# Even projection: each odd tile is turned one product later, and the mixer's first inputs are loaded by the projection

## The reference

```
def ssd_diffattn_mixer(u, w_in, w_out, conv_w, conv_b, ...):
    z, xBC, dt, q, k, v, g = jnp.split(u @ w_in, idx, axis=-1)
    xBC = jax.nn.silu(causal_dwconv(xBC, conv_w, conv_b))
    xs, Bm, Cm = jnp.split(xBC, [SSD_WIDTH, SSD_WIDTH + SSD_GROUPS * SSD_STATE], axis=-1)
    ...
    y = ssd_scan(xs, dt, A, Bm, Cm) + xs * D_skip[:, None]
    y_a = rmsnorm(y * jax.nn.silu(z), ssd_norm_w)
    ...
```

## Time and profile before

| | us |
|---|---|
| median of 3 runs | 4179.75 |
| lowest and highest | 4172.42, 4181.28 |
| the profiled execution | 4173.78 |
| its span | 4172.1 |
| PE busy in it | 3789.3 (91%) |
| DVE, ACT, POOL busy | 2280.9, 1805.1, 1562.0 |
| granted TensorE clock, mean | 0.952 of full |

### The profile page before, as it was taken

How to read it: one execution, slowest core, us unless ns; L and a number is a source line. 1 busy time by engine, 2 the same in 40 slices (tenths; PEclk the granted TensorE clock), 3 DMA queues, 4 the chain that set the end, 5 groups by cost and what they waited for, 6 DMA issues and landing times. The chain is left out here.

```text
span 4172.1 us, 53128 instructions
## 1 busy us (share of the span) xinstructions
PE 3789.3 (91%) x20012; PEld 3213.1 (77%) x20012; DVE 2280.9 (55%) x3708; ACT 1805.1 (43%) x3299; POOL 1562.0 (37%) x1331
## 2 busy tenths in 40 slices
PE   7899777798999999999999878779999999999888
PEld 6667656676888778788777766667799999999876
DVE  6569683426444423312666567743367776777523
ACT  3145555415333323321444358853445455545532
POOL 1422220033444344211234451114366666666333
PEclk9879888899999999999999999899999999999999
DMA  3222301453222264421235587735211111111054
GB/s 147 85 85 70 110 14 38 154 199 106 80 88 79 75 211 157 147 83 69 64 121 156 165 188 128 139 129 164 81 41 50 38 49 44 46 42 50 13 192 146
DMA packets 311658, 421.65 MB, mean 101 GB/s; under 512 B 41755, under 2 KB 213308, under 8 KB 310876
## 3 DMA queue, kind: packets, MB, share of 16 engines
q1 hardware_dynamic: 270556, 291.88, 22.6%
q0 software_dynamic: 38544, 122.18, 10.1%
q10 hardware_dynamic: 2304, 4.20, 0.3%
HBM read 302.04 MB, written 116.15 MB: 100 GB/s over the span
## 5 line engine op out<-in xcount | busy, mean ns | idle before, releaser
L119 PE MATMUL hg_acc<-l_first_ws,l_XT 128*128 128x256 f32 x2880 | 359.6, 284 | 0.0
L119 PEld LDWEIGHTS hg_acc<-l_first_ws,l_XT 128*128 128x128 f32 x2880 | 348.8, 192 | 0.0
L119 PE MATMUL hg_acc<-l_XT,hg_ws 128*128 128x512 f32 x1440 | 343.1, 394 | 0.0
L119 PEld LDWEIGHTS hg_acc<-l_XT,hg_ws 128*128 128x128 f32 x1440 | 266.7, 189 | 52.5
L4404 POOL TENSOR_TENSOR hg_DD<-hg_BB 128x256 f32<-128x256 f32 x224 | 174.0, 777 | 259.9 <-PE hg_pA L4163 133.3
L4261 DVE TENSOR_TENSOR hg_DD<-hg_Q,hg_DD 128x256 f32<-128x256 f32 x224 | 204.6, 914 | 73.3 <-ACT hg_DD L4332 73.2
L119 PE MATMUL even_bank<-l_first_ws,l_XT 128*128 128x512 f32 x888 | 206.2, 390 | 3.2 <-PEq L742 1.9
L119 PE MATMUL even_bank<-even_ws,l_XT 128*128 128x512 f32 x876 | 207.2, 394 | 0.0
L119 PEld LDWEIGHTS even_bank<-l_first_ws,l_XT 128*128 128x128 f32 x888 | 166.2, 188 | 40.7 <-issue 6.0
L119 PEld LDWEIGHTS even_bank<-even_ws,l_XT 128*128 128x128 f32 x876 | 165.2, 190 | 34.3
L119 PE MATMUL am_g_acc<-l_XT,am_ws 128*128 128x512 f32 x768 | 179.0, 395 | 8.9 <-ACT am_stage L1866 8.9
(11 more groups left out here) (677 smaller groups left out, 9288.6 us busy)
## 6 DMA issues: line engine op xcount, KB each, us to landing
l_first_raw<-in_odd_w_in SPq DMA_DIRECT2D x62, 512.0 KB, 5.1
out_first_w<-in_w_ffn_down SPq DMA_DIRECT2D x44, 512.0 KB, 4.0
l_first_raw<-in_even_w_in SPq DMA_DIRECT2D x16, 1024.0 KB, 5.6
out_first_w<-in_even_w_out SPq DMA_DIRECT2D x32, 512.0 KB, 4.5
l_first_raw<-in_odd_w_out SPq DMA_DIRECT2D x32, 512.0 KB, 4.3
da_first_X<-q_k_hi POOLq DMA_DIRECT2D x24, 512.0 KB, 7.5
da_first_X<-q_k_lo POOLq DMA_DIRECT2D x24, 512.0 KB, 12.3
out_first_a<-hidden SPq DMA_DIRECT2D x44, 256.0 KB, 3.0
```

The source lines that it names most:

```text
L119: mm = pe.matmul(out, lhs(p, k), rhs(q, k), start=start and i == 0, stop=stop and i == n - 1, skip_group_check=skip)
```

## The change

Four edits:

1. PE turns the odd tiles one product later: turn(2c - 1) stands behind P4 of pair c and not in front of it. ACT's keep(2c - 1) goes one product later too, from P4 to P3.
2. `y`, the one-hot table `oh` and `lp` get their room in a new tile of 10 KB per partition, `ssd_early_first`, that is allocated before the projection and given back after the mixer (the stage in front of it uses it as `sq`). `y` in the listings below is therefore called `ssd_early_first`.
3. `lower`, the lower parts of the q and k pairs, moves from the room of `y` to that of `x`. DVE's first part waits for the last convolution and not for the stores of `y`.
4. Behind its last load of weights SP waits until b_c and x_b are stored and then loads the mixer's first BC and X into the same tile (`load_first`). The mixer no longer loads them.

```diff
@@ ssd_early_first, allocated in build_program
+        early = Place(nc, "ssd_early").__enter__()
+        first_loads = early.sb("first", [P, 2 * G2 * P + XB2])
...
@@ even_inputs
-        y = pl.sb("y", [P, 2, L])
+        y = mixer.early[:, 0:2 * L].rearrange("p (a n) -> p a n", a=2)
...
-        lower = y[:, :, :].rearrange("p a n -> p (a n)").bitcast(F32R).rearrange("p (b n) -> p b n", b=B)
+        lower = x[:, :, :].rearrange("p a n -> p (a n)")[:, 0:B * NC].bitcast(F32R).rearrange("p (b n) -> p b n", b=B)
@@ its SP queue, behind the loads of the pairs
+                for s in range(2):
+                    sp.wait_ge(f_st[s], (CONV_TILES - FEATURES) // 2 * DMA)
+                    sp.wait_ge(t_st[s], TOKEN_TILES // 2 * DMA)
+                mixer.load_first(sp)
@@ its PE queue
                     if name == "P5" and 1 <= c and 2 * c - 2 < TOKEN_TILES:
                         turn(2 * c - 2)
-                    if name == "P1" and 2 <= c and 2 * c - 3 < TOKEN_TILES:
-                        turn(2 * c - 3)
+                    if name == "P4" and 1 <= c and 2 * c - 1 < TOKEN_TILES:
+                        turn(2 * c - 1)
@@ its ACT queue
                     if name == "P7" and 1 <= c and 2 * c - 2 < TOKEN_TILES:
                         keep(2 * c - 2)
-                    if name == "P4" and 1 <= c and 2 * c - 1 < TOKEN_TILES:
+                    if name == "P3" and 1 <= c and 2 * c - 1 < TOKEN_TILES:
                         keep(2 * c - 1)
@@ its DVE queue, part()
                     if c == CONVED:
-                        dve.wait_ge(f_st[b // 2], (CONV_TILES - FEATURES) // 2 * DMA)
+                        dve.wait_ge(conved, CONV_TILES)
@@ MixerStart
+    def load_first(self, sp):
+        sp.dma_start(self.first_b_c, self.bcT[:, 0:P].rearrange("(g n) l -> n g l", n=P)).then_inc(self.bc_ld, DMA)
+        sp.dma_start(self.first_inputs, self.xbt[0:P, 0:XB2]).then_inc(self.x_ld, DMA)
@@ ssd_mixer
-        X = pl.sb("X", [P, NS, XB2])
-        BC = pl.sb("BC", [P, NS, 2 * G2, P])
+        X = [mixer.first_inputs] + [pl.sb(f"X{s}", [P, XB2]) for s in range(1, NS)]
+        BC = [mixer.first_b_c] + [pl.sb(f"BC{s}", [P, 2 * G2, P]) for s in range(1, NS)]
...
-                load_b_c(0)
-                load_inputs(0)
                 load_b_c(1)
                 load_inputs(1)
                 load_gate(0)
```

More of the change, by code:

```diff
@@ L684, in _, with reduce_tokens @@
                             [wide_of(q) for q in pw(S_T - 1 - s)], shape, at0=ss.half)
-def reduce_tokens(nc, tag, AT, W, res, out, g, begun, turns=None, XT=None, pre=None, after=()):
+def reduce_tokens(nc, tag, AT, W, res, out, g, begun, turns=None, XT=None, pre=None, after=(), room=None):
     K = W.shape[0]
@@ L702, in reduce_tokens @@
         y = pl.sb("y", [P, TT, D])
-        sq = pl.sb("sq", [P, D])
+        sq = pl.sb("sq", [P, D]) if room is None else room
         st = pl.sb("st", [P, 4, TT])
@@ L2547, in even_inputs @@
         tab = pl.sb("tab", [BUCKETS + 1, D_H])
-        oh = pl.sb("oh", [BUCKETS + 1, SKEW])
+        oh = mixer.early[0:BUCKETS + 1, 2 * L:2 * L + SKEW]
         lv = pl.sb("lv", [P, 4, D_QK])
-        lp = pl.sb("lp", [P, 2, D_QK])
+        lp = mixer.early[:, 2 * L + SKEW:2 * L + SKEW + 2 * D_QK].rearrange("p (a n) -> p a n", a=2)
         ls = pl.sb("ls", [P, 4])
@@ L3115, with __init__ @@
 class MixerStart:
-    def __init__(self, nc, tag, dt_bias, A_log, D_skip):
+    def __init__(self, nc, tag, dt_bias, A_log, D_skip, early, xbt, bcT):
+        self.early, self.xbt, self.bcT = early, xbt, bcT
+        self.first_b_c = early[:, 0:2 * G2 * P].rearrange("p (g l) -> p g l", g=2 * G2)
+        self.first_inputs = early[:, 2 * G2 * P:2 * G2 * P + XB2]
         self.place = pl = Place(nc, tag).__enter__()
@@ L3271, in ssd_mixer @@
         pT = pl.ps("pT", [P, 4, P])
-        x_ld = [pl.sem(f"inputs_loaded{s}") for s in range(NS)]
-        bc_ld = [pl.sem(f"b_c_loaded{s}") for s in range(NS)]
+        x_ld = [mixer.x_ld] + [pl.sem(f"inputs_loaded{s}") for s in range(1, NS)]
+        bc_ld = [mixer.bc_ld] + [pl.sem(f"b_c_loaded{s}") for s in range(1, NS)]
         z_ld = [pl.sem(f"gate_loaded{s}") for s in range(NS)]
@@ L3312, in load_b_c @@
                         sp.wait_ge(yo, c - NS + 1)
-                    sp.dma_start(BC[:, s, :, :], bcT[:, c * P:(c + 1) * P].rearrange("(g n) l -> n g l", n=P)).then_inc(bc_ld[s], DMA)
+                    sp.dma_start(BC[s][:, :, :], bcT[:, c * P:(c + 1) * P].rearrange("(g n) l -> n g l", n=P)).then_inc(bc_ld[s], DMA)
                 def load_inputs(c):
@@ L3319, in load_inputs @@
                         sp.wait_ge(ns, c - NS + 1)
-                    sp.dma_start(X[:, s, :], xbt[c * P:(c + 1) * P, 0:XB2]).then_inc(x_ld[s], DMA)
+                    sp.dma_start(X[s][:, :], xbt[c * P:(c + 1) * P, 0:XB2]).then_inc(x_ld[s], DMA)
                 def load_gate(c):
@@ L3396, in keys @@
                     for g in range(G2):
-                        mm = pe.matmul(pCB[:, g, :], BC[:, s, g, :], BC[:, s, G2 + g, :], start=True, stop=True,
+                        mm = pe.matmul(pCB[:, g, :], BC[s][:, g, :], BC[s][:, G2 + g, :], start=True, stop=True,
                                        skip_group_check=True)
@@ L3414, in off_diagonal @@
                     for g in range(G2):
-                        mm = pe.matmul(pYo[:, g * 256:(g + 1) * 256], BC[:, c % NS, G2 + g, :], ST[:, g * 256:(g + 1) * 256],
+                        mm = pe.matmul(pYo[:, g * 256:(g + 1) * 256], BC[c % NS][:, G2 + g, :], ST[:, g * 256:(g + 1) * 256],
                                        start=True, stop=True, skip_group_check=True)
@@ L3433, in new_state @@
                     for g in range(G2):
-                        mm = pe.matmul(pYo[:, g * 256:(g + 1) * 256], X[:, c % NS, X2 + g * P:X2 + (g + 1) * P],
+                        mm = pe.matmul(pYo[:, g * 256:(g + 1) * 256], X[c % NS][:, X2 + g * P:X2 + (g + 1) * P],
                                        Xs[:, g * 256:(g + 1) * 256], start=True, stop=True, skip_group_check=True)
@@ L4511, in build_program @@
             pre = FirstChunk(pl, NC, [e[:, Z_AT:Z_AT + NC]])
-            reduce_tokens(nc, "down", hT, a["w_ffn_down"][0], x1, x2, a["norm_w_2"][0], begun, (ident, ident), XT, pre, stored)
+            reduce_tokens(nc, "down", hT, a["w_ffn_down"][0], x1, x2, a["norm_w_2"][0], begun, (ident, ident), XT, pre, stored, first_loads[:, 0:D])
             begun.close()
             out1_first.close()
-            mixer = MixerStart(nc, "ssd_first", a["dt_bias_2"][0], a["A_log_2"][0], a["D_skip_2"][0])
+            mixer = MixerStart(nc, "ssd_first", a["dt_bias_2"][0], a["A_log_2"][0], a["D_skip_2"][0],
+                               first_loads, xbt, bcT)
             even_inputs(nc, "even", XT, pre, (
```

7 lines of the change are left out of this document (5 added, 2 removed).

## The result

| | before | after |
|---|---|---|
| runs, median (lowest to highest), us | 4: 4178.99 (4172.42 to 4181.28) | 4: 4153.14 (4145.49 to 4163.03) |
| ratio, 95% interval | | 0.9948, 0.9936 to 0.9960 |
| the profiled execution, its span, us | 4173.78, 4172.1 | 4154.62, 4152.9 |
| granted clock, mean | 0.952 | 0.953 |

The changed kernel is faster by 0.5%.

A forecast was written before the change was run, and what follows sets the result against it. PE, busy for 91% of the span, was taken to bound the kernel. Gains of 12.5 + 3.2 + 0.6 + 3.4 = 19.7 us off the 4179.75 us median gave 4160 us, range 4149 to 4173.

The forecast's parts named there:

- Part 1: Odd turns of pairs 1 to 6: PE's six waits for ACT's keep vanish behind P4, 12.5 us, bounds 0 to 12.5.
- The slack: Time between keep's end and the odd turn once waits are gone: 1.8 us in pairs 2 to 6, 0.9 in pair 1.
- The chain: From P4's end through DVE's convolutions and splits, POOL's sums and ACT to the even keep's end: 19.44 us.
- The clock: Falls to 1.2 GHz behind two of six odd-turn waits vanish: 3.2 us, 1.6 each, bounds 0 to 9.6.
- Part 2: Lower parts moved into x's room cost nothing; PE's 4.2 us wait at pair 8's P7 shrinks by 0.6 us.
- the slow stretch: P7 of pair 8 at the slow clock, 5.43 us, expected to stay since 3.6 us of wait remain.
- Part 3: Mixer start: with early loads PE waits only for POOL's small copy, 3.4 us gained, bounds 1 to 5.
- Rival C: Mixer's second chunk waits for inputs at DMA's limit, leaving 0.5 of 3.4 us; 4163 us, chance 0.08.
- The total: All gains together, 19.7 us, taken off the median before to give 4160 us.
- B: Odd-turn waits partly return as the chain over DVE and POOL lengthens; 11.9 us gained, 4168 us, chance 0.14.
- D: P4 and odd turn only swap, PE waits as long for something else, mixer gain lost; 4180 us, chance 0.06.
- E: Slower: the recurrence's 900 us get a clock of 0.97, losing 27 us; 4187 us, chance 0.04.

The follow-up runs named there:

- the turn alone: Kernel before with only the odd turn moved behind P4 and the odd keep behind P3; ratio 0.9946 to the kernel before.
- Even keep at the next P1: Changed kernel with ACT's even keep moved behind its move and rounding for the next pair's P1; 4162.10 us.
- even keep behind P4: Changed kernel with ACT's even keep moved behind what ACT does for P4; 4162.19 us.
- the two experiments: Changed kernel with the old order of turns and keeps, ratio 0.9986 to before; changed kernel with first loads issued at the mixer's start, 4152.41 us.
- even keep first: Kernel before with ACT's even keep put ahead of the rounding that waits for POOL, PE's order untouched; ratio 0.9961 to the kernel before.
- quarter later: Changed kernel with the first upper part of pair 8 moved behind ACT's work for P6; ratios 0.9931 and 0.9937 to the kernel before.
- turn and rooms: Changed kernel with the mixer's first loads issued at the mixer's start again, into their new places; 4152.41 us.

## Why the prediction was right

**Part 1, the wait.** Right in its mechanism; all six waits went, and the turn alone brings nearly the whole gain. Its size was too small, and what was measured lies above the upper bound of 12.5 us that the prediction gave. From P1's start to P3's start pair 2 took 2070.91 - 2062.26 = 8.65 us before and 2068.34 - 2062.02 = 6.32 us after: 2.33 us, where the row of the wait had 2.07. The rest is 0.15 us in the product behind the turn (P4 takes 2.88 us from start to start before; a product that follows a product, as P1 to P4 after, takes 2064.75 - 2062.02 = 2.73), 0.08 us because the idle time is counted from the matmul's end of 2.88 us while the next instruction otherwise starts 2.80 us after it, and 0.03 us in the turn. Over six waits the loss was 13.9 us (17.05 less two falls of 1.57) and not 12.5.

**The slack.** Forecast 1.8 us in pairs 2 to 6 and 0.9 in pair 1, measured 1.4 to 1.6 and 0.55. The chain was forecast well: 19.44 us, and from one odd turn's start to the next keep's end it takes 2066.15 - 2046.51 = 19.64 us up to pair 2 and 19.5 in each pair behind it. What was too long is the pair: 21.22 us had been worked out with the listed wait taken off, and the list is 0.2 us short for each wait; from odd turn to odd turn a pair takes 21.04 us at pair 2 and 20.9 to 21.05 behind it. Nothing became late. "Even keep at the next P1" shows the chain when the slack is used up, and "even keep behind P4" what happens when it is exceeded.

**The clock.** The term of 3.2 us was right for the execution that it was worked out for: six waits at pair 2's 2.33 us and two falls of 1.57 us make 17.1 us, and 17.05 were measured. That it could be 0 to 9.6 us in another was right as a bound; seen were 2, 2, 3 and 2 slow turns of six in the four profiles with the waits, 3.2 to 4.8 us. No odd turn was slow in the eight profiles without such a wait, nor in the one with a single wait of 0.8 us.

**Part 2, pair 8.** 0.68 us for 0.6. Leaving the slow stretch in was right for the profiled execution (5.46 us), but not for the reason given, that a wait of 3.6 us is more than enough for a fall: the same 3.50 us were followed by 3.04 us with the turn alone and 3.05 with the even keep behind P4, by 4.39 with the keep at P1, and by 5.46 in four others. So this term was anything from 0 to 2.4 us in like executions, and that it stayed in the profiled one was luck. (The 3.04 us of a P7 in pair 2 that the prediction compares with is P4's row. P7's own row there has 3.01 us, so nothing hangs on it.)

**Part 3, the first loads.** 3.42 us for 3.4, 3.5 and 3.8 us in the two experiments. Rival C fell: the second chunk's keys come 2353.54 - 2339.98 = 13.56 us behind the first's, 13.47 before, without a wait. PE's first 5.0 us of the mixer ran at 0.50 again, as the prediction left them.

**The total.** 21.15 us in the stretch, for 19.7. The medians differ by 25.9 us and the profiled executions by 19.2. What lies between is outside the stretch: start to first turn took 2031.5 to 2041.9 us over all the profiles, and from the mixer's first matmul to the end 1809.0 to 1817.0 us, in code that no kernel here changes. In two later comparisons the medians differ by 21.1 us each: 4173.76 and 4152.62 for the turn alone, which has 17.3 us in the stretch, or 19.7 where P7 is not slow, and 4174.13 and 4153.04 for the changed kernel. The forecast of 4160 took the sum of an execution off the median; a sum of 21.15 would have given 4158.6. The other 5 us are spread of the few runs, as far as these runs show.

**Rivals.** B and C are ruled out by the rows above, D by PE's waits. E, a later clock, did not come: 1812.9 us after the mixer's start for 1813.1.

## What to carry to other kernels

When an engine waits for a short job of another, look at what stands in front of that job in its queue. If it stands behind a wait that it does not need, either move it ahead of that wait (even keep first, quarter later) or give the waiting engine independent work that lasts until the job ends (the turn behind P4); both took away the same waits, and the second needs slack that can be worked out from the length of a period less the length of the chain. Judge an edit worth 0.5% by the stretch that it touches, start to start on the bounding engine, and not by single times. Here the stretch repeated to 0.4 us between executions with as many slow turns and the same P7, while the times of the changed kernel lay up to 17.5 us apart.

## What the runs showed of the hardware that was not expected

- A wait of PE of 2.0 to 2.2 us was followed by 1.2 GHz in two or three of six like cases, in another set of pairs in each of four profiles; one of 3.50 us in five of seven profiles, and one of 4.2 us in all four profiles that had it. A fall costs about 1.6 us at a turn and its product, up to 2.4 us at P7.
- The idle time listed for a wait of PE is smaller than what the wait costs: 12.5 us listed for six, 13.9 lost, and 13.3 listed for six, 14.4 lost.
- Loads of 512 KB and 768 KB, issued 53 us early beside the stage's last products, delayed nothing that the profile shows: from P7 of pair 8 to the product of PE's last listed wait in the stage it takes 140.80 us with them and 140.87 without (turn and rooms).
